# Hyena filters with channels on partitions: row sums taken by ACT, and PE transposes ahead of the DFT

## The reference, cut to what matters

```python
def hyena_filters(L, w1, b1, freq, w2, b2, w3):
    ...                                  # z: (L, 33) features of the position
    h = jnp.sin(fr * (z @ w1 + b1))
    h = jnp.sin(fr * (h @ w2 + b2))
    h = (h @ w3).reshape(L, HY_ORDER, 2, HY_WIDTH)         # 2 directions, 512 channels
    h = h * jnp.exp(-t[:, :, None, None] * jnp.abs(deltas))
    h = h * lax.rsqrt(jnp.sum(h * h, axis=0, keepdims=True) + EPS)
    h_fwd, h_bwd = h[:, :, 0], h[:, :, 1]
    circ = jnp.concatenate([h_fwd, jnp.zeros_like(h_fwd[:1]), h_bwd[1:][::-1]], axis=0)
    return jnp.fft.rfft(circ, axis=0)
```

## Time and profile before

| what | value |
|---|---|
| median of 3 runs | 3447.09 us (3443.27 to 3451.55) |
| span of the profiled execution | 3444.4 us, its own time as the page gives it |
| PE busy over the span | 2847.6 us (83%) |
| DVE, ACT, POOL busy over the span | 902.5, 604.1, 445.7 us |
| prepare stage | about 33.3 to 384.1 us of the span |

### The profile page before, as it was taken

One profiled execution on the slowest core, in us unless ns is written; L12 is line 12 of the kernel. 1 busy time (PEld: TensorE's weight loads), 2 busy tenths in 40 slices (PEclk: granted clock), 3 DMA queues, 4 the chain that ended last, 5 costly groups with the idle time before them and its releaser, 6 DMA issues. The chain is left out here.

```text
span 3444.4 us, 36314 instructions
## 1 busy us (share of the span) xinstructions
PE 2847.6 (83%) x13347; PEld 1712.4 (50%) x13347; DVE 902.5 (26%) x1677; ACT 604.1 (18%) x1110; POOL 445.7 (13%) x464
## 2 busy tenths in 40 slices
PE   6889698799999997488888849699999839888884
PEld 2233465556565656255555434556644435555553
DVE  2444224614420012311111131614400131111113
ACT  1111121014310002011111122013300101111111
POOL 0321200100000000222222100100000012222221
PEclk7666699999999997699999959899999869999995
DMA  8454211100102205299999831100123229999992
GB/s 282 147 183 152 81 61 55 59 3 8 41 19 55 85 0 225 87 394 394 388 384 376 314 126 61 67 16 10 41 55 104 116 87 397 387 379 389 381 354 76
DMA packets 206810, 589.01 MB, mean 171 GB/s; under 512 B 48322, under 2 KB 104933, under 8 KB 156424
## 3 DMA queue, kind: packets, MB, share of 16 engines
q1 hardware_dynamic: 183144, 556.40, 43.5%
q0 software_dynamic: 21120, 21.04, 2.0%
q10 hardware_dynamic: 2464, 10.49, 0.8%
HBM read 577.29 MB, written 56.68 MB: 184 GB/s over the span
## 5 line engine op out<-in xcount | busy, mean ns | idle before, releaser
L1722 PE MATMUL ps<-wgu,moe_xt 128*64 128x256 f32 x4096 | 513.4, 407 | 160.3 <-DMA wd<-in_w_down_e 158.0
L1722 PEld LDWEIGHTS ps<-wgu,moe_xt 128*64 128x64 f32 x4096 | 341.7, 146 | 290.0 <-issue 178.1
L1318 PE MATMUL ps<-u,w_merge 128*128 128x512 f32 (+1 forms) x768 | 283.7, 528 | 4.1 <-DVEq L1335 4.1
L1730 PE MATMUL ps<-wd,moe_ht 128*64 128x512 f32 x1024 | 247.8, 605 | 1.5 <-DVE moe_ht L1895 1.5
L1889 DVE TENSOR_TENSOR moe_h<-ps,moe_sg 64x256 f32<-64x256 f32 x128 | 54.5, 426 | 682.3 <-ACT moe_sg L1872 675.7
L682 PE MATMUL ps<-u,w_hy 128*128 128x512 f32 (+1 forms) x576 | 212.8, 528 | 18.9 <-PEq L122 18.9
L1802 POOL DMA_INDIRECT rows_out<-moe_y,table x128 | 118.6, 926 | 818.0 <-DVE moe_y L1853 805.5
L1318 PEld LDWEIGHTS ps<-u,w_merge 128*128 128x128 f32 x768 | 147.5, 192 | 135.9 <-issue 124.8
L1738 PE MATMUL ps<-ident,moe_xg 64*128 64x64 f32 x1024 | 140.0, 277 | 75.1 <-DMA moe_xg<-rows_in,table 75.1
L1738 PEld LDWEIGHTS ps<-ident,moe_xg 64*128 64x128 f32 x1024 | 122.5, 199 | 123.9 <-issue 123.9
L682 PEld LDWEIGHTS ps<-u,w_hy 128*128 128x128 f32 x576 | 109.5, 193 | 113.6 <-issue 109.1
(11 more groups left out here) (291 smaller groups left out, 3470.5 us busy)
## 6 DMA issues: line engine op xcount, KB each, us to landing
wgu<-in_w_gate_e SPq DMA_DIRECT2D x128, 1024.0 KB
wgu<-in_w_up_e SPq DMA_DIRECT2D x128, 1024.0 KB
wd<-in_w_down_e SPq DMA_DIRECT2D x128, 1024.0 KB
prep_w<-in_w_ada SPq DMA_DIRECT2D x24, 2048.0 KB, 15.5
w_merge<-in_w_in SPq DMA_DIRECT2D x32, 512.0 KB, 5.1
w_hy<-in_w_in SPq DMA_DIRECT2D x6, 2048.0 KB, 11.4
transfer<-prep_out ACTq DMA_DIRECT2D x10, 1024.0 KB, 5.6
rows_in<-route_utok SPq DMA_DIRECT2D x20, 512.0 KB, 3.6
```

The costliest lines, as they stand in the source:

```text
L1318: last = nc.tensor.matmul(m.ps[:, bank, 0:n], w[:, b, w_at + c], z[:, c, at:at + n], start=c == 0, stop=c == kn - 1)
L1722: last = nc.tensor.matmul(ps[k * SLOTS:(k + 1) * SLOTS, 0:DE], xt[:, c], wgu[:, k, c], start=c == 0, stop=c == KC - 1)
L1730: last = nc.tensor.matmul(ps[k * SLOTS:(k + 1) * SLOTS, 0:512], ht[:, c], wd[:, c, k * 512:(k + 1) * 512], start=c == 0, stop=c == 1)
```

## The change

Channels go on partitions in place of positions. The taps of an item are made as 8 pieces (2 directions, 4 blocks of 128 channels), each 128 channels by all positions of the item, with `w3` as the weights and `h` streamed. The decay is stored turned over (channels by positions). The sum over positions is then a sum along the free axis: ACT squares a piece and its accumulator gives one number for each channel, so the matmul with ones is gone and the inverse norm works on 128x8 elements. ACT scales the backward taps (`backward`), DVE scales the forward ones, adds, puts in the bias, and forms the difference (`combine`). As the DFT needs positions on partitions, PE then turns the sum and the difference by 128x128 transposes, four to a bank (`turn`): 8 banks for a long item, 4 for a short one. ACT and DVE copy these out in turns (`turned_out`). Taps and transposes share two banks, numbers 2 and 3. POOL does no arithmetic; it issues the stores. The bias comes in through two row loads in the load stage, in place of two small loads later.

```diff
-        out[f"decay_{name}"] = np.exp(-t * deltas[None, :])[order].astype(f)
+        out[f"decay_{name}"] = np.ascontiguousarray(np.exp(-t * deltas[None, :])[order].T.astype(f))
...
             def taps(k):
+                for g in range(NF):
+                    n = place["taps", k, g]
+                    bank_free(n)
+                    e, q = divmod(g, HC)
+                    at = (2 * o + e) * HW + q * P
+                    nc.tensor.matmul(m.ps[:, bank(n), 0:lengths[k]], s["w3"][of_layer(l), at:at + P],
+                                     s["h"][of_layer(l), t * SEQ:t * SEQ + lengths[k]], start=True, stop=True).then_inc(s["h3_done"], 1)
+            def turn(k):
+                pe.wait_ge(s["taps_done"], k + 1)
+                for g in range(2 * tiles[k]):
+                    n = place["turn", k, g]
+                    bank_free(n)
+                    part, j = divmod(g, tiles[k])
+                    for q in range(HC):
+                        last = nc.tensor.transpose(m.ps[:, bank(n), q * P:(q + 1) * P], taps_of[:, k % 2, part, q, j * P:(j + 1) * P], m.ident[:])
+                    last.then_inc(s["tr_done"], 1)
...
+                turn(k)
                 if k + 1 < NI:
                     taps(k + 1)
-                if k < NI - 1:
-                    transform(k)
+                transform(k)
                 adas(k + 3)
...
             def squares(k):
+                for g in range(NF):
+                    e, q = divmod(g, HC)
+                    act.wait_ge(s["f_done"], NF * k + g + 1)
+                    if NF * k + g >= 2:
+                        act.wait_ge(s["sq_done"], NF * k + g - 1)
+                    nc.scalar.activation(s["sq"][:, g % 2, 0:lengths[k]], taps_of[:, k % 2, e, q, 0:lengths[k]], ACT.Square,
+                                         accum_out=ss[:, k % 2, g:g + 1]).then_inc(s["sq_done"], 1)
...
+            def backward(k):
+                act.wait_ge(s["inverse_done"], k + 1)
+                for q in range(HC):
+                    b = taps_of[:, k % 2, 1, q, 0:lengths[k]]
+                    nc.scalar.mul(b, b, rn[:, k % 2, HC + q:HC + q + 1]).then_inc(s["t_done"], 1)
+            def turned_out(k):
                 if k:
+                    act.wait_ge(s["sin_done"], first_unit[k])
+                    act.wait_ge(s["cos_done"], first_unit[k])
+                for g in range(0, 2 * tiles[k], 2):
+                    part, j = divmod(g, tiles[k])
+                    act.wait_ge(s["tr_done"], turned[k] + g + 1)
+                    nc.scalar.activation(f[:, part, j], m.ps[:, bank(place["turn", k, g])], ACT.Copy).then_inc(s["tr_evac_a"], 1)
...
         def _(pool):
+            for unit, (k, j) in enumerate(units):
+                i, l, t, o = items[k]
+                pool.wait_ge(s["cos_folded"], unit + 1)
+                pool.wait_ge(s["sin_folded"], unit + 1)
+                pool.dma_start(dram["h"][l][t][o, :, :, j], out[:, unit % 2]).then_inc(h_out[unit % 2], 16)
+            for r in range(2):
+                pool.wait_ge(h_out[r], 16 * (len(units) // 2))
...
+            def combine(k):
+                i, l, t, o = items[k]
+                g, n, col = taps_of[:, k % 2], lengths[k], R_FB + o * HC
+                for q in range(HC):
+                    dve.wait_ge(s["t_done"], HC * k + q + 1)
+                    last = nc.vector.scalar_tensor_tensor(g[:, 0, q, 0:n], g[:, 0, q, 0:n], rn[:, k % 2, q:q + 1], g[:, 1, q, 0:n], ALU.mult, ALU.add)
+                link(last)
+                link(nc.vector.tensor_tensor(g[:, 0, :, 0], g[:, 0, :, 0], m.cols[:, l, col:col + HC], ALU.add))
+                nc.vector.scalar_tensor_tensor(g[:, 1, :, 0:n], g[:, 1, :, 0:n], -2.0, g[:, 0, :, 0:n], ALU.mult, ALU.add).then_inc(s["taps_done"], 1)
+            def turned_out(k):
+                if k:
+                    dve.wait_ge(s["sin_done"], first_unit[k])
+                    dve.wait_ge(s["cos_done"], first_unit[k])
+                for g in range(1, 2 * tiles[k], 2):
+                    part, j = divmod(g, tiles[k])
+                    dve.wait_ge(s["tr_done"], turned[k] + g + 1)
+                    nc.vector.tensor_copy(f[:, part, j], m.ps[:, bank(place["turn", k, g])]).then_inc(s["tr_evac_v"], 1)
...
             decayed(0)
-            for k in range(NI + 1):
-                if k >= 1:
-                    if k < NI:
-                        decayed(k)
-                    difference(k - 1)
-                    fold(k - 1)
-                if k < NI:
-                    inverse_norm(k)
+            inverse_norm(0)
+            combine(0)
+            for k in range(NI):
+                turned_out(k)
+                if k + 1 < NI:
+                    decayed(k + 1)
+                fold(first_unit[k])
+                if k + 1 < NI:
+                    inverse_norm(k + 1)
+                    combine(k + 1)
+                for unit in range(first_unit[k] + 1, first_unit[k + 1]):
+                    fold(unit)
```

More of the change, by code:

```diff
@@ L290, in prepare_stage, with bank @@
         loaded, h_out = [s[f"ada{k}_in"] for k in range(RING)], [s["h0_out"], s["h1_out"]]
-        f, sq, var, rn, out = s["f"], s["sq"], s["var"], s["rn"], s["out"]
-        angle, turn = (b[:].rearrange("p e n -> p (e n)")[:, 0:TOK] for b in (var, sq))
+        taps_of, f, out, ss, rn = s["g"], s["f"], s["out"], s["ss"], s["rn"]
+        angle, turns = (out[:, i].rearrange("p a b n -> p (a b n)")[:, 0:TOK] for i in range(2))
+        def bank(n):
+            return 2 + n % 2
         def ada_wait(eng, g):
@@ L336, in adas, with bank_free @@
                 ada_columns(slots[slot][-1])
+            def bank_free(n):
+                if n < 2:
+                    return
+                kind, k, g = shared[n - 2]
+                if kind == "taps":
+                    pe.wait_ge(s["f_done"], NF * k + g + 1)
+                elif g % 2 == 0:
+                    pe.wait_ge(s["tr_evac_a"], (turned[k] + g) // 2 + 1)
+                else:
+                    pe.wait_ge(s["tr_evac_v"], (turned[k] + g) // 2 + 1)
             def taps(k):
@@ L362, in transform @@
                 J, dft = tiles[k] // 2, s[f"dft{t}"]
[L363 to L364 removed]
+                pe.wait_ge(s["tr_evac_a"], turned[k + 1] // 2)
+                pe.wait_ge(s["tr_evac_v"], turned[k + 1] // 2)
                 for j in range(J):
@@ L408, in root @@
             def root(k):
                 act.wait_ge(s["var_done"], k + 1)
[L410 to L426 removed]
+                nc.scalar.activation(rn[:, k % 2], s["var"][:], ACT.Sqrt).then_inc(s["root_done"], 1)
@@ L428, in evacuate, with others @@
+            def others(unit):
+                for part, done, folded in ((0, "cos_done", "cos_folded"), (1, "sin_done", "sin_folded")):
+                    act.wait_ge(s[done], unit + 1)
+                    if unit >= 1:
+                        act.wait_ge(s[folded], unit)
+                    nc.scalar.activation(s["other"][:, part], m.ps[:, 6 + part], ACT.Copy).then_inc(s["other_done"], 1)
             def evacuate(g):
@@ L488, in decayed @@
                 i, l, t, o = items[k]
-                J = tiles[k]
                 if k >= 2:
-                    n = sum(item <= k - 2 for item, _ in units)
-                    dve.wait_ge(s["cos_done"], n)
-                    dve.wait_ge(s["sin_done"], n)
-                for q in range(2 * J):
-                    e, j = divmod(q, J)
-                    dve.wait_ge(s["h3_done"], 2 * before[k] + q + 1)
-                    nc.vector.tensor_tensor(f[:, k % 2, e, j], m.ps[:, q % 2], s[f"decay{t}"][:, j], ALU.mult).then_inc(s["f_done"], 1)
+                    dve.wait_ge(s["tr_done"], turned[k - 1])
@@ L499, in inverse_norm @@
+                for g in range(NF):
+                    e, q = divmod(g, HC)
+                    dve.wait_ge(s["h3_done"], NF * k + g + 1)
+                    nc.vector.tensor_tensor(taps_of[:, k % 2, e, q, 0:lengths[k]], m.ps[:, bank(place["taps", k, g]), 0:lengths[k]],
+                                            s[f"decay{t}"][:, q], ALU.mult).then_inc(s["f_done"], 1)
             def inverse_norm(k):
-                dve.wait_ge(s["sum_done"], 2 * before[k + 1])
-                nc.vector.tensor_scalar_add(var[:], m.ps[:, 2:4], EPS).then_inc(s["var_done"], 1)
+                r = rn[:, k % 2]
@@ new lines, in turned_out, with fold @@
+            def turned_out(k):
[6 more added lines that the diff above has]
+                    nc.vector.tensor_copy(f[:, part, j], m.ps[:, bank(place["turn", k, g])]).then_inc(s["tr_evac_v"], 1)
+            def fold(unit):
+                if unit >= 2:
+                    dve.wait_ge(h_out[unit % 2], 16 * (unit // 2))
+                for part, done, folded in ((0, "cos_done", "cos_folded"), (1, "sin_done", "sin_folded")):
+                    dve.wait_ge(s[done], unit + 1)
+                    dve.wait_ge(s["other_done"], 2 * unit + part + 1)
```

(5 more changed lines are left out.)

123 lines of the change are left out of this document (36 added, 87 removed).

## The result

The changed kernel takes 3322.37 us (median of 4 runs, 3315.7 to 3332.8) against 3446.22 us for the one before. The ratio is 0.9639, with a 95% interval from 0.9621 to 0.9657. The profiled execution has a span of 3325.3 us, 119.1 less than before.

What follows compares the result with a forecast made beforehand. PE was taken to set the filter stage's length, through its clock as much as its work. Terms -80.2 + 34.8 - 21.4 + 1.5 - 19.2 - 5.1 = -89.6 us gave 3354.8, plus 2.7 for the median: 3357 us, range 3338 to 3396.

Steps and rivals of the forecast that it cites:

- the rest of the kernel keeps its length: Outside the filter stage: nothing changes but its place in time; the span of 3444.4 us less the stage stays.
- Sums -80.2: Filter stage on PE: all 40 matmul sums over positions go, saving 80.2 us.
- Transposes +34.8: New PE turns: four long at 6.9 us and two short at 3.6 us add 34.8 us.
- Taps -21.4: PE tap matmuls: 55.4 us against 76.8, at full clock behind long turns and half clock in item 0.
- Filter-chain waits -19.2: PE waits on the filter chain: 24.2 us vanish, 5.0 us of idle PE appear in item 0.
- Short slots +1.5: Short iterations: PE waits for ACT's modulation row copies queued behind `backward`, 1.5 us over both.
- End of stage -5.1: After the last DFT: modulation covers the last store, leaving 2.2 us before the next stage, saving 5.1 us.
- the likeliest case: Whole kernel: the forecast of 3357 us, with its own range 3343 to 3370 and a chance of 0.52.
- Taps at 1.2 GHz: Rival: taps stay at half clock, whole (3392 us) or in part (about 3377 us); chance 0.26.
- Nearly full clock throughout: Rival: filter stage almost all at full clock, taps 47 and turns 30 us, giving -103 us, 3344; chance 0.10.
- The longer chain: Rival: the DVE and ACT chain outlasts its cover, giving back 40 us, 3397; chance 0.08.
- the stores by POOL: Rival: DVE's fold waits for POOL-issued stores, making the kernel slower than before, past 3447 us; chance 0.03.

Runs made afterwards that it cites:

- second pair of profiles: The kernel before and the changed kernel each run again unchanged for a second trace: 3447.76 and 3328.78 us.
- the reverse shift: Changed kernel with 64 unused bytes per partition ahead of the expert weight rings, in the expert stages alone: 3350.11 us, ratio 0.9721.
- the run with short sums: Kernel before, with 56 of the 80 sum-of-squares matmul records run over 8 columns instead of 512, waits kept: 3420.51 us, ratio 0.9919.
- The run with 128 rows: Changed kernel with tap matmuls over all 128 rows instead of 64, the other layer's rows held at zero: 3312.20 us, ratio 0.9605.
- the kernel with 128 rows and early modulation rows: Changed kernel with 128-row taps, and ACT copying modulation rows ahead of the backward scaling in item 0 and short items: 3307.42 us, ratio 0.9596.

## Why the prediction was wrong, step by step

*"Nothing outside the stage is touched by more than its place in time, so the rest of the kernel keeps its length."* This step failed, and it is most of the miss of 35 us. The rest is 22.4 us shorter (19.2 in the second pair of profiles); 17.5 of that came with 64 bytes of shift and no other edit, and the reverse shift took it back. The wider `m.cols` is a part of the change, and with it the shift of every later address; the forecast counted its loads and not its place. The remaining 2 to 5 us are about what two profiles of one kernel differ by (3 us) and stay open. Of the other 12.6 us of the miss, 7.0 are the stage, below, and 5.6 are this: the forecast put the median 2.7 us above the profiled span, as before, and it came 2.9 below it, within the spread of the four runs.

*The stage* was forecast at -89.6 us and gave -96.6. Term by term:

- Sums -80.2: gone as forecast. That they were worth their full length fits the run with short sums, where the waits stayed and the gain did not come in full.
- Transposes +34.8: measured 31.3, and 1.7 of waits for copies between them, 33.0. The short turns took 3.1 us, entered with the clock still up, and 3.9 at half (forecast 3.6), the long ones 6.2 to 6.9 (forecast 6.9). The forecast let the long turns enter at half clock; of all six only those of items 3 and 4 did. The clock rose within a turn (at 83.0 us, and in the turn at 218.07). The Trainium skill's rule in "TensorE: Matmul & The Clock Gate", Part 4, that transposes don't engage the full clock, does not hold in this kernel.
- Taps -21.4: measured 55.2 against 76.8, -21.6. The sum is right, its parts partly by luck: item 0 took 13.6 and not 15.5, item 4 took 14.0 and not 12. The forecast gave every instruction with a wait a break of 0.29 us. Each of these matmuls has a wait for its bank, and item 0's ran at 1.70 us each, without a break. So the wait alone does not make the break of the old steps; what does is open.
- Filter-chain waits -19.2: 24.2 us went, and in place of the 5.0 us that I left ahead of item 0's turn stands 1.04. The chain after the last fold took 7.3 us (101.9 to 109.2 in item 1), forecast 8.0, and the slot that covers it in item 0 took 9.1 us (68.8 to 77.8) where 5.8 were forecast: its first block ran partly at half clock, and 1.51 us of it are a wait for rows. The cover was longer by luck.
- Short slots +1.5: PE waited 1.96 and 2.81 us for the rows, but before it had waited 6.1 for such rows too, against 6.3 now: about 0.
- DFT and modulation were left at their length. At the higher mean clock the DFT fell by 0.8 us (68.8 to 68.0) and modulation, with the two lines of before below, by 2.4 (68.3 to 65.9).
- End of stage -5.1: from PE's last column at 285.1 to the norm it is 2.4 us, before 7.4: -5.0.

```profile
L317 PE MATMUL ps<-prep_w,sil 128*32 128x512 f32 x320 | 43.5, 683 | 2.6 <-ACT mod L437 1.8 <-DMA prep_w<-in_w_ada 0.8
L327 PE MATMUL ps<-prep_sel,prep_rows 128*128 128x2 f32 x160 | 24.8, 283 | 6.1 <-ACT prep_rows L432 6.1
```

These add up to some -100 us and not to -96.6, because neighbouring records overlap (the groups add up to 5.8 us more than PE's busy time before, to 3.0 more after) and the first taps began 0.9 us later. PE took 229.9 us from first taps to its end, forecast 238. The stage is 7 us better than forecast; with the rest at its length the time would have been about 3350 us (3446.2 - 96.6), inside the likeliest case's own range.

*The rivals.* Taps at 1.2 GHz: half true. They never raised the clock themselves (13.61, 7.34, 14.02 us) but held it (7.70, 7.77). The run with 128 rows shows that it is the 64 rows. Nearly full clock throughout came true only in the kernel with 128 rows and early modulation rows: a stage end of 257.6 us, 30 before the change's. The longer chain and the stores by POOL did not occur; no DVE fold waited for a store.

## What to carry to other kernels

When an edit changes the size of an on-chip buffer, compute where every later buffer that a DMA streams into now starts: here a start at a multiple of 256 bytes was worth some 18 us in two stages bound by weight loads. Pad for it on purpose, and compare kernels at equal placement before crediting an edit. Where TensorE alternates between short pieces and waits, a saving need not be worth its length: here 39 us of shortened sums gave 24, and moving three waits, for 0.9 us less of idle time, gave 12.2, as the granted clock moved too. Watch that clock stretch by stretch.

## What the runs showed of the hardware

- The rate at which expert weights land depended on their start on chip: in the middle of the first expert stage 385 to 387 GB/s at 64 or 192 past a multiple of 256 bytes, 388 at 128 past it, 391 to 393 at a multiple of 256, and 393 at one of 512.
- Fp32 matmuls on 64 rows, back to back for 13.5 us, stayed at a granted clock of 0.50, and the same columns on 128 rows reached full clock within 9.2 us. Once full clock was granted, 64 rows held it for 7.7 us.
- The clock rose while TensorE did only transposes: 0.50 from 79.8 to 82.8 us and 1.00 from 83.1 to 85.0 in one turn, 0.50 from 218.1 to 222.5 and 1.00 from 223.0 to 224.9 in another, and 1.00 in the taps behind both.
- One record (half) of an fp32 matmul with 8 columns took 0.29 us where one with 512 took 1.0, so cutting columns to a sixty-fourth left more than a quarter of the time.
